# RMS norms of a two-layer hybrid step: row statistics with tokens on the partitions in place of statistics repeated on all partitions

## The reference

```python
def rmsnorm(x, g):
    y = x * lax.rsqrt(jnp.mean(x * x, axis=-1, keepdims=True) + EPS)
    return y * g

def run_layer(x, mod, attn_fn, lp):
    shift1, scale1, gate1, shift2, scale2, gate2 = jnp.split(mod, 6, axis=-1)
    h = modulate(rmsnorm(x, lp['norm1_g']), shift1, scale1)
    mix, kv = token_mixers(h, attn_fn, lp)          # projections, four branches, output projection
    x = x + gate1 * mix
    h2 = modulate(rmsnorm(x, lp['norm2_g']), shift2, scale2)
    return x + gate2 * expert_choice_ffn(h2, ...), kv   # router logits, top-k, 16 experts
```

## Time and profile before

| | |
|---|---|
| median of 3 runs | 2743.27 us (2742.66 to 2746.19) |
| the profiled execution, its own time | 2747.89 us |
| its span | 2746.1 us |
| TensorE busy | 2543.1 us (93%) |
| TensorE weight loads | 1936.7 us (71%) |
| VectorE busy | 1166.4 us (42%) |
| GpSimd busy | 980.0 us (36%) |
| ScalarE busy | 818.5 us (30%) |
| mean granted TensorE clock | 0.974 of full |

### The profile page before, as it was taken

The page is one execution under the profiler, slowest core; times in us unless marked ns, Lnnn a source line. Parts: engine busy times, 40 slices in busy tenths (PEclk is TensorE's granted clock), DMA queues, the critical chain, the costliest instruction groups (busy, mean ns, idle before and its releaser), DMA issues.

```text
span 2746.1 us, 80150 instructions
## 1 busy us (share of the span) xinstructions
PE 2543.1 (93%) x31510; PEld 1936.7 (71%) x31510; DVE 1166.4 (42%) x2033; ACT 818.5 (30%) x3460; POOL 980.0 (36%) x2992
## 2 busy tenths in 40 slices
PE   6998999999997899999789999999999959999995
PEld 3555676666745899888746566776666559998984
DVE  3997534665425011111268874356653331111114
ACT  3112223443213443333021132334331233333320
POOL 2373233232201255445435633133221014454453
PEclk9999999999998999999989999999999979999998
DMA  8332311212236899999633322211132249999993
GB/s 328 120 131 92 110 57 53 75 53 105 80 122 267 345 427 428 428 427 427 274 130 123 130 92 90 75 49 64 61 138 83 105 178 396 428 427 428 428 428 134
DMA packets 43854, 572.39 MB, mean 208 GB/s; under 512 B 5248, under 2 KB 5376, under 8 KB 8320
## 3 DMA queue, kind: packets, MB, share of 16 engines
q1 hardware_dynamic: 40032, 550.52, 49.5%
q10 hardware_dynamic: 2592, 16.38, 1.5%
q0 software_dynamic: 1024, 3.15, 0.4%
HBM read 561.11 MB, written 8.91 MB: 208 GB/s over the span
## 4 chain that ended last, share of the span: by engine, by line
PE 63%; DMA 22%; DVE 11%; issue 2%; ACT 1%; DVEq 0%; POOL 0%; ACTq 0%; POOLq 0%; SPq 0%
PE ps L462 47%; DMA ring<-in_w_exp 12%; PE ps L629 6%; DMA region_b<-in_w_exp 6%; DVE region_b L1659 5%; DMA region_x<-in_w_exp 4%; PE ps L884 3%; PE ps L850 1%; PE ps L833 1%; PE ps L821 1%; PE ps L996 1%; DVE region_r L1948 0%; DVE rstd L1573 0%; DVE region_r L1947 0%; ACT region_r L2274 0%
## 5 line engine op out<-in xcount | busy, mean ns | idle before, releaser
L2266 POOL TENSOR_TENSOR region_m<-region_m,region_r 128x8 f32 x2416 | 433.2, 221 | 559.6 <-DVE region_r L1987 504.9
L462 PE MATMUL ps<-region_r,ring 128*64 128x80 f32 x12096 | 445.8, 234 | 30.4 <-DMA ring<-in_w_exp 17.2
L462 PEld LDWEIGHTS ps<-region_r,ring 128*64 128x64 f32 x12096 | 434.2, 138 | 40.3 <-issue 22.5
L462 PE MATMUL ps<-hT,ring 128*128 128x320 f32 (+2 forms) x1440 | 431.6, 442 | 8.2 <-ACT hT L1169 8.2
L2274 ACT ACTIVATE region_r<-hT 128x8 f32 x2410 | 292.0, 204 | 281.7 <-DVE region_r L1999 153.3
L462 PEld LDWEIGHTS ps<-hT,ring 128*128 128x128 f32 x1440 | 257.7, 192 | 146.9 <-issue 68.3
L462 PE MATMUL ps<-region_r,region_b 128*64 128x80 f32 x8064 | 298.2, 235 | 42.3 <-DMA region_b<-in_w_exp 20.7
L462 PEld LDWEIGHTS ps<-region_r,region_b 128*64 128x64 f32 x8064 | 290.6, 138 | 49.3 <-DVE region_r L2276 18.7
L1659 DVE SCALAR_TENSOR_TENSOR region_b<-region_b,params 128x655 f32<-128x655 f32 x240 | 278.0, 1158 | 8.5
L462 PE MATMUL ps<-region_b,ring 128*128 128x320 f32 x560 | 182.5, 435 | 0.0
L462 PE MATMUL ps<-region_r,region_x 128*64 128x80 f32 x4032 | 152.3, 237 | 16.0 <-DMA region_x<-in_w_exp 8.3
(11 more groups left out here) (281 smaller groups left out, 3425.6 us busy)
## 6 DMA issues: line engine op xcount, KB each, us to landing
ring<-in_w_exp SPq DMA_DIRECT2D x90, 2048.0 KB, 24.7
region_b<-in_w_exp SPq DMA_DIRECT2D x60, 2048.0 KB, 24.6
ring<-in_w_mix SPq DMA_DIRECT2D x39, 2048.0 KB, 8.1
region_x<-in_w_exp SPq DMA_DIRECT2D x30, 2048.0 KB, 24.7
ring<-in_w_pair SPq DMA_DIRECT2D x32, 1536.0 KB, 6.3
region_b<-in_w_first SPq DMA_DIRECT2D x4, 2048.0 KB, 13.8
ring<-in_w_ada SPq DMA_DIRECT2D x4, 2048.0 KB, 10.0
ring<-in_w_first SPq DMA_DIRECT2D x3, 2048.0 KB, 11.6
```

The costliest lines, as they stand in the source:

```text
L462: ins = pe.matmul(*args, **kw)
L2266: last = eng.tensor_tensor(x[:, :, token], x[:, :, token], y_gated[e % 2][:, :, c:c + 1], ALU.add)
```

## The change

For all norms but ("in", 0), the squares become the weights and a single column of ones the moving operand, so that each matmul yields 128 sums, one to a partition, for 128 tokens. Five (or four) such columns hold all tokens. For an "in" norm the four steps write separate columns, 20 in all, and VectorE reduces them by four. Variance, root and reciprocal then run on 128x5 (or 128x4) in a new small tile, `tok_root`. A new function, `norm_spread`, multiplies each column, broadcast along the free axis, with the identity, which puts the inverse roots on all partitions of a PSUM tile (`spread`). The products that make h read this PSUM tile instead of the SBUF tile `rstd`. In a layer's second norm the spreading stands in TensorE's queue behind context tile 1; in the others it stands right behind the sums. A new semaphore in each direction (`root_inverse`, `norm_spread`) ties VectorE and TensorE.

```diff
--- before.py
+++ after.py
@@ -353,6 +353,8 @@
         index = region_r[0:NE, 1536:1536 + CAP].bitcast(I32)
         slot_gate = rstd[0:CAP, 80:80 + NE]
         rt_max, rt_sum = small[:, 56:61], small[:, 61:66]
+        tok_root = small[:, 68:73]
+        spread = {"in": PS[3][:, :, 0:HALF], "mix": PS[2][:, 0, :]}
 
 
         slot_loaded = [sem(f"slot_loaded{i}") for i in range(len(slots))]
@@ -363,7 +365,7 @@
         stored, kv_stored, bias_in = sem("stored"), sem("kv_stored"), sem("bias_in")
         out_ready = sem("out_ready")
         names = """x_stored x_back params_in cache_in dve_step pool_step
-            squared square_used norm_sum var_ready root_ready xr_ready h_ready hc_ready ada_rows ada_row_in ada_turned ada_part_in ada_half mod_sum mod_ready
+            squared square_used norm_sum norm_spread var_ready root_ready root_inverse xr_ready h_ready hc_ready ada_rows ada_row_in ada_turned ada_part_in ada_half mod_sum mod_ready
             tile_done conv_sig conv_in pool_in u_ready zv_ready q_in k_in v_in
             pads_zero conv_summed conv_mean conv_centred conv_var conv_norm conv_ready
             pool_d poolw_done pool_ready sgu_norm sgu_mixed sgu_ready turned roped
@@ -486,7 +488,10 @@
             def norm_sum(key):
                 if key[0] == "mix":
                     pe.wait_ge(S["square_used"], ADD_AT[key] + KC - 1)
-                    mm(PS[2][:, 0, :], ones, rstd[:, 0:LAT], start=True, stop=True).then_inc(S["norm_sum"], 1)
+                    for t in range(LAT // P):
+                        last = (pe.matmul if t else mm)(PS[2][:, 0, t:t + 1], rstd[:, t * P:(t + 1) * P], ones[:, 0:1],
+                                                        start=True, stop=True)
+                    last.then_inc(S["norm_sum"], 1)
                     return
                 if key[1] == 0:
                     pe.wait_ge(S["square_used"], ADD_AT[key] + KC - 1)
@@ -496,9 +501,23 @@
                 need = needs(pe, key[1] - 1)
                 for step, (name, n, k) in enumerate((("sq_dve", 1, 5), ("sq_act", 3, 2), ("sq_pool", 1, 1), ("sq_sum", 1, 7))):
                     need(name, n)
-                    for b, t0, t1 in columns("half"):
-                        last = (pe.matmul if step else mm)(PS[1][:, b, 0:t1 - t0], ones, x_sq[:, k, t0:t1], start=step == 0, stop=step == 3)
+                    for t in range(TT):
+                        last = (pe.matmul if step or t else mm)(
+                            PS[1][:, 0, 4 * t + step:4 * t + step + 1], x_sq[:, k, t * P:(t + 1) * P], ones[:, 0:1],
+                            start=True, stop=True)
                 last.then_inc(S["norm_sum"], 1)
+
+            def norm_spread(key):
+
+                cuts = [(t, 0, P) for t in range(LAT // P)] if key[0] == "mix" else \
+                    [(0, 0, P), (1, 0, P), (2, 0, P // 2), (2, P // 2, P), (3, 0, P), (4, 0, P)]
+                pe.wait_ge(S["root_inverse"], NORM_AT[key])
+                for t, c0, c1 in cuts:
+                    at = t * P + c0
+                    out = PS[2][:, 0, at:at + c1 - c0] if key[0] == "mix" else \
+                        PS[3][:, at // HALF, at % HALF:at % HALF + c1 - c0]
+                    last = pe.matmul(out, tok_root[:, t:t + 1].broadcast_to([P, P]), ident[:, c0:c1], start=True, stop=True)
+                last.then_inc(S["norm_spread"], 1)
 
             def h_chunk(where, l, k):
 
@@ -1005,6 +1024,8 @@
                             merged[:, k, LAT:TOK], start=k == 0, stop=k == KC - 1)
                     if m == 0:
                         norm_sum(("mix", l))
+                    if m == 1:
+                        norm_spread(("mix", l))
                     if m % 4 == 3:
                         last.then_inc(S["ctx_out_done"], 1)
                         read(block_at["out", m // 4])
@@ -1132,6 +1153,7 @@
                     expert_block(FIRST_BLOCKS + LOOP_BLOCKS + b, 0, y_ps, act, "y_done")
 
                 norm_sum(("in", l + 1))
+                norm_spread(("in", l + 1))
                 assert not pending
 
             pe.wait_ge(cond_ready, 1)
@@ -1490,7 +1512,7 @@
                 for k in range(KC):
                     need("x_mixed", k + 1)
                     square(("mix", l), k, x[:, k, 0:LAT], LAT)
-                root(3 * l + 3, rstd[:, 0:LAT])
+                root(3 * l + 3, tok_root[:, 0:LAT // P])
                 for k in range(KC):
                     sc.wait_ge(S["mod_ready"], mods(l, 1, k))
                     sc.wait_ge(S["xr_ready"], KC * NORM_AT["mix", l] + k + 1)
@@ -1548,7 +1570,7 @@
                 need("x_ready", 2)
                 for k in range(5):
                     sc.activation(x_sq[:, k, :], x[:, k, :], ACT.Square).then_inc(S["sq_act"], 1)
-                root(3 * l + 4, rstd[:, 0:TOK])
+                root(3 * l + 4, tok_root)
 
             for l in range(LAYERS):
                 layer(l)
@@ -1566,16 +1588,31 @@
             def inverse_root(key, roots):
 
                 v.wait_ge(S["norm_sum"], NORM_AT[key] + 1)
-                ps = PS[1] if key[0] == "in" and key[1] else PS[2]
-                inc(v.tensor_scalar(rstd[:, 0:TOK].rearrange("p (b t) -> p b t", b=2), ps[:, :, 0:HALF],
-                                    1.0 / D, EPS, ALU.mult, ALU.add), "var_ready")
+                if key == ("in", 0):
+                    inc(v.tensor_scalar(rstd[:, 0:TOK].rearrange("p (b t) -> p b t", b=2), PS[2][:, :, 0:HALF],
+                                        1.0 / D, EPS, ALU.mult, ALU.add), "var_ready")
+                    v.wait_ge(S["root_ready"], roots)
+                    link(v.reciprocal(rstd[:, 0:TOK], rstd[:, 0:TOK]))
+                    return
+                n, ps = (TT, PS[1]) if key[0] == "in" else (LAT // P, PS[2])
+                total = ps[:, 0, 0:n]
+                if n == TT:
+                    total = tok_root
+                    link(v.tensor_reduce(total, ps[:, 0, 0:4 * n].rearrange("p (t s) -> p t s", s=4), AX, ALU.add))
+                inc(v.tensor_scalar(tok_root[:, 0:n], total, 1.0 / D, EPS, ALU.mult, ALU.add), "var_ready")
                 v.wait_ge(S["root_ready"], roots)
-                link(v.reciprocal(rstd[:, 0:TOK], rstd[:, 0:TOK]))
+                v.reciprocal(tok_root[:, 0:n], tok_root[:, 0:n]).then_inc(S["root_inverse"], 1)
+                v.wait_ge(S["norm_spread"], NORM_AT[key])
+
+            def halves(ap):
+
+                return ap.rearrange("p (b t) -> p b t", b=2)
 
             def normalise(key, roots):
 
                 inverse_root(key, roots)
-                normalised(0, KC)
+                for k in range(KC):
+                    v.tensor_tensor(halves(h[:, k, :]), halves(x[:, k, :]), spread["in"], ALU.mult).then_inc(S["xr_ready"], 1)
 
             def normalised(k0, k1):
                 for k in range(k0, k1):
@@ -1901,12 +1938,9 @@
                     if m >= 2:
                         add_square(("mix", l), m - 1, LAT)
                 add_square(("mix", l), KC - 1, LAT)
-                v.wait_ge(S["norm_sum"], NORM_AT["mix", l] + 1)
-                inc(v.tensor_scalar(rstd[:, 0:LAT], PS[2][:, 0, :], 1.0 / D, EPS, ALU.mult, ALU.add), "var_ready")
-                v.wait_ge(S["root_ready"], 4 * l + 4)
-                link(v.reciprocal(rstd[:, 0:LAT], rstd[:, 0:LAT]))
+                inverse_root(("mix", l), 4 * l + 4)
                 for k in range(KC):
-                    v.tensor_tensor(h[:, k, 0:LAT], x[:, k, 0:LAT], rstd[:, 0:LAT], ALU.mult).then_inc(S["xr_ready"], 1)
+                    v.tensor_tensor(h[:, k, 0:LAT], x[:, k, 0:LAT], spread["mix"], ALU.mult).then_inc(S["xr_ready"], 1)
                 mix_context(0)
                 mix_context(1)
 
@@ -2031,7 +2065,7 @@
                 layer(l)
             inverse_root(("in", LAYERS), 4 * LAYERS + 1)
             for k in range(KC):
-                v.scalar_tensor_tensor(h[:, k, :], x[:, k, :], con("final_g", KC)[:, k:k + 1], rstd[:, 0:TOK],
+                v.scalar_tensor_tensor(halves(h[:, k, :]), halves(x[:, k, :]), con("final_g", KC)[:, k:k + 1], spread["in"],
                                        ALU.mult, ALU.mult).then_inc(out_ready, 1)
```

## The result

The changed kernel took 2772.45 us in the median of 10 runs (2753.93 to 2777.98), the kernel before, run beside it, 2745.93 (10 runs, 2742.66 to 2749.48): ratio 1.0077, 95% interval 1.0059 to 1.0094 (it goes by the means, 2766.8 and 2745.6; the medians lie 26.5 us apart). That is slower by 0.8%, where the prediction said 2744.0 and, in its range, at most 2748.5. The changed kernel's times also lie in two groups, 4 runs at 2754 to 2759 and 6 at 2772 to 2778. The profiled execution has a span of 2770.8 us, 24.7 more than before.

A forecast was written before the change was run, and what follows sets the result against it. TensorE and its weight loads were taken to bound the kernel. Terms +1.75 + (1.95 - 2.0) + (1.6 - 2.0) - 0.5 = +0.8 us on 2743.27 gave about 2744.0 us, 8-in-10 range 2737.5 to 2748.5.

The forecast's parts named there:

- The expert stage gives none of it back: Expert stage after each layer's inner norm: recovers nothing of the later router logits, so each such norm's +0.88 us stays.
- the 0.08 for slower: Whole kernel: the chance given to a result slower by over 0.2%.
- Norms inside the layers: Norm inside each layer: sums exchange at 0, spreading matmuls add 0.88 us without a stall; +1.75 for two.
- Rivals 4 and 5: Clock falls at norms inside layers, 2747.5 us, chance 0.08; those norms were on the path after all, 2738, chance 0.03.
- Sums at the half clock: Norms between layers and at the end: 40 one-column passes keep the clock at half, sums later by 1.95 and 1.6 us.
- rival 1: Clock rises during the one-column sums as before: 2738.4 us, or 2735.6 if it stays up into the projection; chance 0.18.
- Rival 2: Norms between layers and at the end: a weight load takes 0.11 us at half clock too; 2740.0 us, chance 0.1.
- Rival 3: One-column passes do not overlap with the next weight load, about 0.42 us each at half clock; 2763 us, chance 0.06.
- Chain after the sums: Norms between layers and at the end: from VectorE's reduction to first product 3.8 us instead of 5.81, -2.0 each.
- Start of the next projection: Projection after the norm between layers: spreading passes may raise the clock sooner, between 0 and -1.7 us, taken as -0.5.
- Products from PSUM: Products that make h: reading one operand from PSUM costs 0, at most 0.06 us for each of the eight last ones.

The follow-up runs named there:

- 18626: Kernel before plus 128 empty TensorE instructions ahead of layer 1's expert loop, putting it where the changed kernel has it: 2771.81 us; with them hidden in waits, 2757.55 us.
- 18620: Kernel before plus 122 hidden empty TensorE instructions ahead of layer 1's expert loop: 2821.47 us, ratio 1.0276.
- residue 194: Kernel before plus 13 empty TensorE instructions ahead of layer 0's first expert matmul, moving layer 0's expert loop within its 256-instruction piece: 2832.85 us, ratio 1.0312.
- 18632: Changed kernel plus 6 empty TensorE instructions ahead of layer 1's first expert matmul, where TensorE waits: 2747.07 us, ratio 1.0004.
- 18658: Changed kernel plus 32 empty TensorE instructions at the start of layer 1, moving its expert loop on: 2745.42 us, ratio 1.0000.
- 18612: Kernel before plus 114 hidden empty TensorE instructions ahead of layer 1's expert loop: 2744.51 us, ratio 0.9994.

## Why the prediction was wrong

**The step that failed** is one sentence: "The expert stage gives none of it back: its first matmuls wait for the slots that VectorE chooses from these logits, and the weight loads are released by TensorE." It took layer 1's expert stage for the same stage, shifted. Its data dependences were the same; its code was not at the same place. The chain of the kernel before has only short pieces of issue there, none over 2 us, and where the loop's code lies was never asked. What the runs showed in its place: TensorE pauses three times at the loop's jump back while code is fetched again, 34.8 us in all, which costs the profiled execution 24.7. None of the five rivals had a mechanism outside the norms, and the 0.08 for slower hung on two mechanisms (one-column passes that don't overlap, a fall of the clock) that both turned out false.

**Shown:** the loop's position makes the pauses. They appear with the old norms (at 18626, 18620 and, in layer 0, residue 194), vanish with the new ones (18632, 18658), come in the other loop when that is moved or lengthened, and q8 brings code behind each. With the pauses gone the changed kernel stands at 1.0000 [0.9991, 1.0009] and 1.0004 [0.9995, 1.0013]. With the piece's end read from the second stops, each of the bad places has its body over eight pieces and each of the good ones over seven; that seven stay and eight don't is shown for these two loops. **Argued only:** that this is the size of a store for code, and not another rule that gives the same places. The Trainium skill ("Advanced Engine Details and Errata", ISA Cache) gives TensorE 128 KB in lines of 16 KB or 256 instructions, which by an estimate from these two figures would be eight lines. The packets' size agrees; the limit found here is seven pieces, one less. It also says that there are only two lines, and "Runtime: NRT & Kernel Launch" (Instruction fetch mechanics) that a taken branch whose target is not in the current two-page window forces a fetch. This case's trace speaks against two: before, a body of over six pieces jumps back 13 times in the 405 us from 2295 to 2700, and there is no packet on q8.

**Open:** why a bad place costs a pause in every second iteration at one start and in every sixth at another, and why the jump takes 7.0 to 8.0 us in every pause, when the first two packets have landed long before (in the first pause at 2324.9, the jump ends at 2326.29). The packets themselves don't fill that time (in the first pause their queue has 2.6% of 16 engines' 10 us, 4.2 us of packets). The wait for the third piece is longer where the weights' queue is full (5.6 and 5.9 us against 3.2), so traffic accounts for part of it, but not for the jump, which is as long in the first pause as in the others. At 18620 TensorE goes on ahead of the third piece, runs two passes and pauses again for 2.53 us, which makes its 7.00 + 2.53 much the same wait as the changed kernel's 10.26: the jump is the same, and the piece ends six instructions later.

**Term by term**, where the mechanisms held:

- Norms inside the layers: +0.88 each predicted, +0.92 measured, twice; no stall at the spreading, clock 1.00 all through. Rivals 4 and 5 are out.
- Sums at the half clock: +1.95 and +1.6 predicted, +2.07 and +1.70 measured. 38 passes in 8.24 us are 0.217 each, against 0.215 assumed. The granted clock was 0.50 to the end of the sums: rival 1 is out. Rival 2 (a load of 0.11 at the half clock, the rule of the Trainium skill, "TensorE: Matmul & The Clock Gate", LDWEIGHTS) is out by the same row, which shows twice that. Rival 3 (0.42 a pass) is out too.
- Chain after the sums: -2.0 each predicted, -1.93 and -1.94 measured.
- Start of the next projection: -0.5 predicted, -0.08 measured. The row is `1388.17 11.22 PE ps L464 x30` against 11.30 in the earlier trace rows; the spreading passes did not bring the clock up before the projection.
- Products from PSUM: 0 predicted; the eight last ones take 6.42 us against 6.46.

Sum of the measured terms +1.7 us, predicted +0.8. The forecast of the local work was right to 0.9 us and the forecast of the kernel wrong by 28, of which 2.7 are its base (2743.27, the median of three runs, against 2745.93).

## What to carry to other kernels

A loop on an engine has a size in code and a place in the program. Where its body is near the number of code pieces that stay resident (here, on TensorE, a body over seven pieces stays and one over eight doesn't), any edit ahead of it can turn pauses on or off, for both kernels of a comparison. So before a change in time is put down to what was changed: look for pauses that wait for "issue" at the head of a loop, count the packets of the instruction queue, and run the kernel once more with a few empty instructions ahead of the loop, at a point where the engine waits anyway. Here this test would have told a change of nothing from a loss of 0.8%, and found a loss of 3% thirteen empty instructions away from the kernel before.

An operation that is short on the vector engines but adds passes on the engine that bounds the kernel is to be used only where the vector engines end last. Of this change's two halves the one between the layers about breaks even, the one inside the layers costs 0.9 us each.

## What was not expected of the hardware

- The same body of code, jumped back to 14 times, runs with no fetch at one place and with seven fetches of nine 16 KB packets at a place 8 instructions further (18612 and 18620: 81 and 144 packets, 2744.51 and 2821.47 us).
- A pause of 10 to 12 us on TensorE cost about 8 us of the kernel's time where it came every sixth iteration (24.7 us for three); a pause of 9 to 10 us cost 11 to 12 where it came every second; the block behind it took 7.3 us (18620) in place of 4.35, at a mean granted clock of 0.59.
- A semaphore increment that nobody waits for takes TensorE 0.15 us, more than a pass of 128 columns at the full clock (0.111).
